# Output projection and gating dealt out among the attention units of the next token tile

## The chip, the cores and the metric

The kernel runs on one core of one Trainium2 chip. A core has TensorE (PE, with its weight loads shown apart as PEld), VectorE (DVE), ScalarE (ACT), GpSimd (POOL) and SyncE (SP), which here only issues transfers. Each engine works through its own instruction stream in order and waits on semaphores. The metric is the device time of one execution in microseconds, the median of several runs.

## The reference, cut to what matters

Two layers of a transformer-like block over 128 context tokens and 512 latent tokens, width 1024. In each layer:

```
mod = silu(cond) @ mod_w + mod_b                  # sh1, sc1, g1, sh2, sc2, g2
h = rms_norm(x, norm1_g) * (1 + sc1) + sh1
... = split_proj(h @ w_in)
o_a = recurrent scan;  o_g = global attention;  o_w = windowed attention with a sink
x = x + g1 * (concatenate([o_a, o_g, o_w]) @ w_out)     # what the change moves
h = rms_norm(x, norm2_g) * (1 + sc2) + sh2
x = x + g2 * moe(h)
```

The modulation rows differ between context (tile 0) and latent tokens (tiles 1 to 4). The context reads only itself; a latent tile's global attention reads five key tiles (four latent, one cached), its windowed attention three or four.

## The kernel before

Everything is float32. The 640 tokens are `NT` = 5 tiles of 128. A layer is one pass of a hardware loop and consists of blocks; all engines meet at a block's end. The block around the change is attention. Its work is 60 units, twelve for each token tile (2 kinds of attention x 2 key heads x 3 query heads), and `U` is 60. The order is written out by hand as steps 0 to 61, and all engines walk the same steps:

- PE (`score_pair`, L1012) on even steps makes the scores of units s and s+1; on each step it turns the probabilities of unit s-1 by transposes (`turn`, L1038) and multiplies those of unit s-2 by the values (`weigh`, L1051).
- DVE takes the row maximum of unit s (`maximum`, L1115 or L1119 with the mask), every four steps normalises a finished group of four units into `oall` (`outputs`, L1149 to L1151), and copies a part of the turned probabilities of unit s-1 out of PSUM (`copy_turned`, L1140). Four pieces of work on the scan's output (`scan_norm`) lie on steps 2, 4, 6 and 8.
- ACT makes the exponentials of unit s (L1081) and copies the other part (`copy_turned`, L1094).
- Before `weigh` begins a new group (steps 6, 10, 14, ..., that is 2 mod 4) PE waits until `outputs` has emptied the one PSUM bank that the groups share.

Eight more pieces of `silu(cond) @ mod_w` (numbers 4 to 11, `mod_rows`, L339, 64 matmuls each) are laid on steps 4, 10, 16, ..., 46 (`mod_at`), between `score_pair` and `turn`, in PSUM banks 6 and 7; DVE adds the bias (`mod_evac`, L1162). SP loads their 2 MB of weights in three buffers, the 4 MB of `w_out`, and at the end stores the finished rows to memory in two transfers, waits, and the block ends.

The next block is the projection. For each tile PE turns `oall` by eight transposes (L1225) into PSUM, ACT copies the 128x1024 result to `oT` (L1247), PE multiplies it by `w_out` in two halves of 512 columns, eight products each (L1237; each float32 product is recorded as two MATMULs, so 32 for a tile). DVE multiplies the 1024 columns with the gate rows `g1b` (L1258) and adds to `x` (L1262). Transposes of tile t+1 go ahead of the products of tile t; `oT`, `prod` and the PSUM banks are double. SP loads `g1b` at the block's start (L1209). The block after it begins with squares of `x` on ACT (L1340).

```
                    for step in range(U + 2):
                        if step < U and step % 2 == 0:
                            score_pair(step)
                        if step in mod_at:
                            ...
                        if 1 <= step <= U:
                            turn(step - 1)
                        if step >= 2:
                            weigh(step - 2)
```

Of the kernel before, what the change touches and what calls it, by code (L numbers as in the profile page):

```python
# [13 lines left out]
ALU = mybir.AluOpType  # L14
# [11 lines left out]
AH = 4  # L26
# [37 lines left out]
def program(nc, x_prompt, x_sample, cgk, cgv, cwk, cwv, state, c, c_ctx, mod_w, mod_b, norm1_g, norm2_g,  # L64
# [4 lines left out]
    with ctx:  # L69
# [89 lines left out]
        assert tt[0] <= scan0 + 6 * TOK  # L159
# [5 lines left out]
        oT = T[:, 0:2 * KC * P].rearrange("p (s k n) -> p s k n", s=2, k=KC)  # L165
        prod = T[:, 2048:2048 + 2 * D].rearrange("p (s n) -> p s n", s=2)
        g1b = T[:, scan0:scan0 + 2 * D].rearrange("p (s n) -> p s n", s=2)
# [120 lines left out]
        with nc.Fori(0, DEPTH) as layer:  # L288
# [29 lines left out]
            def by_group(a, cond):  # L318

                return a[cond:P:32]  # L320
# [98 lines left out]
            with nc.Block() as block:  # L419
# [504 lines left out]
            s_row2, s_mst, s_wo, s_hp, s_hq, s_hn, s_fill = (  # L924
                lsem(n) for n in ("mod_bias_load2", "mod_rows_stored", "wout_load", "scan_mean", "scan_rstd", "scan_norm",
# [39 lines left out]
            mod_at = {4 + 6 * i: MOD1 + i for i in range(NMOD - MOD1)}  # L965

            with nc.Block() as block:
                @block.sync
                def _(sp):
# [15 lines left out]
                    for cond in range(2):  # L985
                        sp.dma_start(mod_dram[cond, :].rearrange("(s g b) -> g s b", g=MODG, b=P),
                                     by_group(modrow2, cond)).then_inc(s_mst, 16)
                    sp.wait_ge(s_mst, 2 * 16)
# [10 lines left out]
                def _(pe):  # L999
# [56 lines left out]
                    for step in range(U + 2):  # L1056
                        if step < U and step % 2 == 0:
                            score_pair(step)
                        if step in mod_at:
                            n = mod_at[step]  # L1060
                            if n >= MOD1 + 2:
                                pe.wait_ge(s_mre, n - 1)
                            mod_rows(pe, n, 6 + n % 2).then_inc(s_mr, 1)
                        if 1 <= step <= U:
                            turn(step - 1)
                        if step >= 2:
                            weigh(step - 2)

                @block.scalar
                def _(act):  # L1070
# [25 lines left out]
                    for step in range(U + 2):  # L1096
                        if step < U:
                            exponential(step)
                        if 1 <= step <= U:
                            copy_turned(step - 1)  # L1100

                @block.vector
                def _(dve):
# [52 lines left out]
                    def mod_evac(n):  # L1156
# [5 lines left out]
                        ins = dve.tensor_tensor(r, PS[:, 6 + n % 2, 0:P], r, ALU.add)  # L1162
# [9 lines left out]
                    def scan_norm(part):  # L1172
# [6 lines left out]
                        elif part == 2:  # L1179
                            flow(dve.tensor_tensor(osum, osum, ga, ALU.mult))  # L1180
                        else:
                            dve.wait_ge(s_hq, 1)
                            flow(dve.tensor_tensor(oall[:, :, 0:AW].rearrange("p t (a d) -> p t a d", d=HD),
                                                   osum.rearrange("p t (a d) -> p t a d", d=HD),
                                                   hrs.unsqueeze(3).to_broadcast([P, NT, AH, HD]), ALU.mult))
# [3 lines left out]
                    for step in range(U + 3):  # L1189
                        if step < U:  # L1190
                            maximum(step)
                        if step >= 3 and (step - 3) % GU == GU - 1:
# [9 lines left out]
            s_gb, s_ot, s_ote, s_y, s_yp, s_yv = (  # L1202
                lsem(n) for n in ("gate_rows_load", "o_turned", "o_turned_evac", "y_done", "y_gated",
                                  "y_added"))

            def load_rows(sp, dst, at, s_sig):

                for cond in range(2):
                    sp.dma_start(dst[:, cond, :], mod_dram[cond, at * D:(at + 1) * D].partition_broadcast(P))\  # L1209
                      .then_inc(s_sig, 16)  # L1210

            with nc.Block() as block:
                @block.sync
                def _(sp):
                    load_rows(sp, g1b, 0, s_gb)

                @block.tensor
                def _(pe):
                    pe.wait_ge(s_wo, 16)

                    def turn(t):
                        if t >= 2:
                            pe.wait_ge(s_ote, t - 1)
                        for k in range(KC):
                            last = pe.transpose(PS[:, 2 * (t % 2) + k // 4, col(k % 4)], oall[:, t, col(k)], ident)  # L1225
                        last.then_inc(s_ot, 1)

                    turn(0)
                    for t in range(NT):
                        if t + 1 < NT:  # L1230
                            turn(t + 1)
                        pe.wait_ge(s_ote, t + 1)
                        if t >= 2:
                            pe.wait_ge(s_yp, t - 1)
                        for b in range(2):
                            for k in range(KC):
                                last = pe.matmul(PS[:, 4 + 2 * (t % 2) + b, :], oT[:, t % 2, k, :],  # L1237
                                                 wout[:, k, col(b, 512)], start=(k == 0), stop=(k == KC - 1))
                        last.then_inc(s_y, 1)

                @block.scalar
                def _(act):
                    for t in range(NT):
                        act.wait_ge(s_ot, t + 1)
                        if t >= 2:
                            act.wait_ge(s_y, t - 1)
                        act.activation(oT[:, t % 2, :, :].rearrange("p k n -> p (k n)"),  # L1247
                                       PS[:, 2 * (t % 2):2 * (t % 2) + 2, :].rearrange("p b n -> p (b n)"),
                                       ACT.Copy).then_inc(s_ote, 1)

                @block.vector
                def _(dve):
                    dve.wait_ge(s_gb, 2 * 16)
                    for t in range(NT):
                        dve.wait_ge(s_y, t + 1)
                        if t >= 2:
                            dve.wait_ge(s_yv, t - 1)
                        dve.tensor_tensor(prod[:, t % 2, :],  # L1258
                                          PS[:, 4 + 2 * (t % 2):6 + 2 * (t % 2), :].rearrange("p b n -> p (b n)"),
                                          g1b[:, 1 if t else 0, :], ALU.mult).then_inc(s_yp, 1)  # L1260
                        dve.wait_ge(s_yp, t + 1)
# [543 lines left out]
```

## Time and profile before

| | us |
|---|---|
| median of three runs (range) | 1830.77 (1828.58 to 1835.3) |
| the profiled execution | 1821.91 |
| span in the profile, first to last instruction | 1819.0 |
| end of the last `weigh` to the start of the next block, layer 1 / 2 | 78.87 / 78.88 |
| units of tile 2, layer 1 | 34.60 |
| units of tile 1, layer 1 | 45.00 |

A line of the timeline gives the start in us from the start of the span, the duration, engine, line, operation, output<-input, shape and count; in brackets stands the idle time of that engine just before, and what ended it. Neighbouring instructions of a kind are merged. The granted clock (PEclk) is the share of TensorE's full 2.4 GHz; it has two levels, 1.00 and 0.50 (1.2 GHz).

### The profile page before, as it was taken

To read this page: it belongs to the slowest core of one execution; us is meant where nothing else is said; L and a number is where in the kernel's file an instruction comes from. 1 tells how busy PE (TensorE), PEld (TensorE's weight loads), DVE (VectorE), ACT (ScalarE), POOL (GpSimd) and SP (SyncE) were. 2 spreads that over 40 slices of the span, in tenths; PEclk is the share of its full clock that TensorE was granted. 3 is DMA by queue.
4 is the path that set the end of the run, shared out by engine and by line. 5 is a ranking of instruction groups with operands and counts; after the bars stand their busy time and mean duration, and the time that the engine had idled before them with its cause. 6 is when DMAs were issued, how large, how long until landed. Compare 5 with 4: busy or idle time off the path is not lost. (4 is left out here: it accounts for less than half of the span.)

```text
span 1819.0 us, 22010 instructions
## 1 busy us (share of the span) xinstructions
PE 1469.5 (81%) x7971; PEld 929.6 (51%) x7972; DVE 625.1 (34%) x1352; ACT 359.4 (20%) x814; POOL 202.1 (11%) x151
## 2 busy tenths in 40 slices
PE   2799999698898559999039999987988964999940
PEld 2466556587753534444035755556877434444410
DVE  0236462545421421111411454635553134111123
ACT  2210012233311301111122000123332030111113
POOL 0114420100000010000210243110000000100010
PEclk9799999579899569999569999997896985999975
DMA  8211000825000369996380111027200034799833
GB/s 307 74 50 50 29 23 2 325 94 220 2 24 14 120 240 351 370 368 239 127 287 11 41 50 47 6 104 267 94 2 24 0 110 171 259 366 370 326 110 117
DMA packets 118648, 263.36 MB, mean 145 GB/s; under 512 B 10120, under 2 KB 27168, under 8 KB 118432
## 3 DMA queue, kind: packets, MB, share of 16 engines
q1 hardware_dynamic: 105600, 214.97, 33.3%
q0 software_dynamic: 8064, 29.36, 4.4%
q10 hardware_dynamic: 4896, 17.83, 2.4%
q8 instruction: 58, 0.95, 0.2%
q14 instruction: 30, 0.25, 0.0%
HBM read 230.88 MB, written 42.27 MB: 150 GB/s over the span
## 5 line engine op out<-in xcount | busy, mean ns | idle before, releaser
L638 PE MATMUL PS<-W,hT 128*128 128x512 f32 (+1 forms) x640 | 274.1, 555 | 0.0
L1587 PE MATMUL PS<-W,T 128*128 128x512 f32 x544 | 242.5, 599 | 4.5 <-ACT T L1629 4.5
L1587 PEld LDWEIGHTS PS<-W,T 128*128 128x128 f32 x544 | 104.3, 193 | 135.7 <-issue 130.0
L1051 PE MATMUL PS<-T 128*128 128x64 f32 x864 | 135.3, 308 | 27.4 <-DVE hT L1151 27.4
L1051 PEld LDWEIGHTS PS<-T 128*128 128x128 f32 x864 | 132.5, 232 | 32.0 <-issue 32.0
L638 PEld LDWEIGHTS PS<-W,hT 128*128 128x128 f32 x640 | 109.9, 189 | 74.5 <-issue 60.3
L1237 PE MATMUL PS<-W,T 128*128 128x512 f32 x320 | 139.7, 596 | 0.0
L1605 PE MATMUL PS<-W,T 128*128 128x512 f32 x272 | 126.0, 607 | 1.4 <-ACT T L1653 1.4
L810 DVE COPY_PREDICATED W<-levelmask,PS 128x512 f32<-128x512 uint8 (+2 forms) x96 | 77.6, 809 | 104.0 <-PE PS L579 103.8
L1012 PE MATMUL PS<-T 64*128 64x128 f32 (+3 forms) x480 | 90.7, 466 | 15.9 <-ACT T L1081 12.7
L542 PE MATMUL PS<-hT,W 128*128 128x512 f32 x192 | 100.3, 604 | 2.6 <-DVE hT L781 2.6
L1038 PE MATMUL PS<-cst,T 128*128 128x128 f32 x432 | 85.3, 324 | 16.3 <-ACT T L1081 8.2
L1237 PEld LDWEIGHTS PS<-W,T 128*128 128x128 f32 x320 | 60.9, 193 | 73.3 <-issue 73.3
L579 PEld LDWEIGHTS PS<-W 64*128 64x128 f32 x1120 | 69.0, 187 | 56.0 <-issue 38.9
L1675 DVE TENSOR_TENSOR T<-PS,T 128x256 f32<-128x256 f32 x34 | 14.5, 426 | 240.3 <-ACT T L1640 240.3
L508 PE MATMUL PS<-cst,T 128*128 128x128 f32 x80 | 19.1, 425 | 84.2 <-ACT T L663 84.2
L1081 ACT ACTIVATE T<-PS,small 128x640 f32<-128x640 f32 (+1 forms) x72 | 46.9, 651 | 194.2 <-DVE small L1126 158.9
L579 PE MATMUL PS<-W 64*128 64x128 f32 x1120 | 85.1, 287 | 0.0
L1115 DVE TENSOR_REDUCE small<-PS 128x1 f32<-128x640 f32 (+1 forms) x72 | 46.5, 646 | 105.5 <-PE PS L1012 105.3
L1671 DVE COPY T<-PS 128x1024 f32<-128x1024 f32 x34 | 41.7, 1226 | 119.4 <-PE PS L1605 119.4
L339 PE MATMUL PS<-W,condT 128*32 128x128 f32 x1536 | 63.0, 334 | 23.6 <-DMA W<-in_mod_w 18.8
L1545 POOL DMA_INDIRECT T<-h_rows,T x36 | 34.0, 944 | 427.7 <-PE PS L1577 323.9
(244 smaller groups left out, 1712.1 us busy)
## 6 DMA issues: line engine op xcount, KB each, us to landing
W<-in_w_gate_up SPq DMA_DIRECT2D x34, 2048.0 KB
W<-in_mod_w SPq DMA_DIRECT2D x24, 2048.0 KB, 12.2
W<-in_w_down SPq DMA_DIRECT2D x34, 1024.0 KB
y_rows<-T ACTq DMA_DIRECT2D x34, 512.0 KB, 9.2
y_rows<-cst SPq DMA_DIRECT2D x2, 7680.0 KB
W<-in_w_in SPq DMA_DIRECT2D x10, 1024.0 KB, 11.0
W<-in_w_in SPq DMA_DIRECT2D x4, 2048.0 KB, 7.9
W<-in_w_out SPq DMA_DIRECT2D x2, 4096.0 KB, 25.6
```

The source lines that it names most:

```text
L339: last = pe.matmul(PS[32 * g:32 * g + 32, bank, 0:P], condT[:, k, :], modw[:, n % 3, k, col(g)], start=(k == 0), stop=(k == KC - 1))
L542: pe.matmul(PS[:, bank, :], w, hT[:, k, 0:512], start=(k == 0), stop=(k == KC - 1))
L579: last = pe.matmul(PS[:, bank + r, col(2 * (tile - t) + f)], k_op[64 * r:64 * r + 64, d, f, col(tile)], rhs, start=True, stop=True)
L638: last = pe.matmul(PS[:, u % 4, 0:512 - at], hT[:, k, col(t)], ring[:, slot, k, at:512], start=(k == 0), stop=(k == KC - 1))
L810: dve.copy_predicated(query_side(Am[:, d, :, t:t + tiles, :, :].rearrange("p r t f n -> p r (t f n)"), lv, d), mask.to_broadcast([P, 4 * t ...
L1012: return pe.matmul(PS[:, score_bank(u) + n // 4, (n % 4) * P:(n % 4 + m) * P], qT[kv_rows, wnd, j, col(t)], kT[kv_rows, wnd, kt * P:(kt + ...
L1038: last = pe.transpose(PS[:, bank, col(at)], pr[units[u][1]][:, col(n)], ident)
L1051: last = pe.matmul(PS[:, 5, in_group(u) * HD:(in_group(u) + 1) * HD], prT[wnd][:, col(n)], v[:, kt, kv * HD:(kv + 1) * HD], start=(n == 0) ...
L1081: act.activation(pr[wnd][:, 0:n], src, ACT.Exp, bias=stat(nbias, u), scale=SCALE, accum_out=stat(rsum, u)).then_inc(s_ax, 1)
L1237: last = pe.matmul(PS[:, 4 + 2 * (t % 2) + b, :], oT[:, t % 2, k, :], wout[:, k, col(b, 512)], start=(k == 0), stop=(k == KC - 1))
L1587: last = pe.matmul(PS[:, 2 + par, :], hgT[:, par, k, :], w[:, k, :], start=(k == 0), stop=(k == KC - 1))
L1605: last = pe.matmul(PS[:, 6 + b, :], haT[:, par, col(f)], w[:, f, col(b, 512)], start=(f == 0), stop=(f == 1))
```

## The change

The projection block is gone. Its work for tile t is put into the steps of the next tile's units, starting at `window[t]` = 12 (t + 1) + 3, so at steps 15, 27, 39, 51 and, for the last tile, 63, after all units:

- `turn_out(t)` at step `window`: eight transposes into banks 6 and 7, and ACT's `copy_out` into the one `oT`, ahead of ACT's `copy_turned` of that step.
- `project(t, 0)` at `window` + 1 and `project(t, 1)` at `window` + 5: eight products each, into bank 6 and bank 7, between `score_pair` and `turn`. These are steps 16, 20; 28, 32; 40, 44; 52, 56; 64, 68.
- `gate_out(t, b)` on DVE at `window` + 5 and `window` + 9, after `maximum` and ahead of `copy_turned`: product and sum of 512 columns each. Steps 20, 24; 32, 36; 44, 48; 56, 60; 68, 72.
- The pieces of the modulation move from steps 4, 10, 16, 22, 28, 34, 40, 46 to 8, 13, 17, 22, 29, 34, 41, 46.
- SP loads `w_out` one place earlier, waits until pieces 4 and 5 are finished, stores those two, waits, loads `g1b`, and only then goes on with the weights of pieces 7 to 11; the other six rows are stored at the end.
- `oT`, `prod` and `g1b` get other places; `oT` and `prod` are single. A new semaphore `s_on` tells that the scan's part of `oall` is written.

```diff
-            mod_at = {4 + 6 * i: MOD1 + i for i in range(NMOD - MOD1)}
+            UT = U // NT
+            window = [UT * (t + 1) + 3 for t in range(NT)]
+            HALF = 4
+            LASTSTEP = window[-1] + 2 * HALF + 1
+            mod_at = {8: MOD1, 13: MOD1 + 1}
+            mod_bank = {MOD1: 6, MOD1 + 1: 7}
+            for i in range(3):
+                mod_at[window[i] + 2], mod_bank[MOD1 + 2 + 2 * i] = MOD1 + 2 + 2 * i, 7
+                mod_at[window[i] + 7], mod_bank[MOD1 + 3 + 2 * i] = MOD1 + 3 + 2 * i, 6
+            turn_at = {window[t]: t for t in range(NT)}
+            part_at = {window[t] + 1 + HALF * b: (t, b) for t in range(NT) for b in range(2)}
+            gated_at = {window[t] + HALF * (b + 1) + 1: (t, b) for t in range(NT) for b in range(2)}
...
                     load_mod(sp, MOD1 + 1)
+                    sp.dma_start(wout[:, :, :], w_out[layer].rearrange("(k p) n -> p k n", p=P)).then_inc(s_wo, 16)
                     load_mod(sp, MOD1 + 2)
-                    sp.dma_start(wout[:, :, :], w_out[layer].rearrange("(k p) n -> p k n", p=P)).then_inc(s_wo, 16)
+                    sp.wait_ge(s_mre, MOD1 + 2)
+                    store_mods(sp, MOD1, 2)
+                    sp.wait_ge(s_mst, 2 * 16)
+                    load_rows(sp, g1b, 0, s_gb)
                     for n in range(MOD1 + 3, NMOD):
                         load_mod(sp, n)
...
+                    def turn_out(t):
+                        pe.wait_ge(s_mre, mods_before(window[t]))
+                        pe.wait_ge(s_aev, G * (t + 1))
+                        if t == 0:
+                            pe.wait_ge(s_on, 1)
+                        else:
+                            pe.wait_ge(s_yp, 2 * t)
+                        for k in range(KC):
+                            last = pe.transpose(PS[:, 6 + k // 4, col(k % 4)], oall[:, t, col(k)], ident)
+                        last.then_inc(s_ot, 1)
+
+                    def project(t, b):
+                        if b == 0:
+                            pe.wait_ge(s_ote, t + 1)
+                            if t == 0:
+                                pe.wait_ge(s_wo, 16)
+                        else:
+                            pe.wait_ge(s_mre, mods_before(window[t] + 5))
+                        for k in range(KC):
+                            last = pe.matmul(PS[:, 6 + b, :], oT[:, k, :], wout[:, k, col(b, 512)],
+                                             start=(k == 0), stop=(k == KC - 1))
+                        last.then_inc(s_y, 1)
...
-                    for step in range(U + 2):
+                    for step in range(LASTSTEP):
                         if step < U and step % 2 == 0:
                             score_pair(step)
+                        if step in turn_at:
+                            turn_out(turn_at[step])
                         if step in mod_at:
-                            n = mod_at[step]
-                            if n >= MOD1 + 2:
-                                pe.wait_ge(s_mre, n - 1)
-                            mod_rows(pe, n, 6 + n % 2).then_inc(s_mr, 1)
+                            mod_side(step)
+                        if step in part_at:
+                            project(*part_at[step])
                         if 1 <= step <= U:
                             turn(step - 1)
...
+                    def gate_out(t, b):
+                        if (t, b) == (0, 0):
+                            dve.wait_ge(s_gb, 2 * 16)
+                        dve.wait_ge(s_y, 2 * t + b + 1)
+                        if t >= 1:
+                            dve.wait_ge(s_yv, 2 * (t - 1) + b + 1)
+                        dve.tensor_tensor(prod[:, b, :], PS[:, 6 + b, :], g1b[:, 1 if t else 0, col(b, 512)], ALU.mult)\
+                           .then_inc(s_yp, 1)
+                        dve.wait_ge(s_yp, 2 * t + b + 1)
+                        dve.tensor_tensor(x[:, t, col(b, 512)], x[:, t, col(b, 512)], prod[:, b, :], ALU.add).then_inc(s_yv, 1)
...
+                        if step in gated_at:
+                            gate_out(*gated_at[step])
                         if step in mod_at:
                             mod_evac(mod_at[step])
                         if 1 <= step <= U:
                             copy_turned(step - 1)
...
-            with nc.Block() as block:
-                @block.sync
-                def _(sp):
-                    load_rows(sp, g1b, 0, s_gb)
...
```

## Rows read from the trace of the kernel before

**Rows 1.** The page: span, and busy time, share and instructions of each engine.

```profile
span 1819.0 us, 22010 instructions
PE 1469.5 (81%) x7971; PEld 929.6 (51%) x7972; DVE 625.1 (34%) x1352; ACT 359.4 (20%) x814; POOL 202.1 (11%) x151
```

**Rows 2.** Windows: stretch, length, busy (x) per engine, granted clock, DMA.

```profile
core 0: us, PE busy (x) PEld busy (x) DVE busy (x) ACT busy (x) POOL busy (x), PEclk, DMA share, GB/s
351.10:396.10 45.00, 41.41 (x326) 35.81 (x327) 18.61 (x58) 12.98 (x39) 0.00 (x0) 0.66 0.40 141
396.10:430.70 34.60, 30.18 (x349) 27.67 (x349) 19.94 (x59) 14.07 (x40) 0.00 (x0) 1.00 0.70 265
...
508.65:587.52 78.87, 74.91 (x200) 35.89 (x200) 13.00 (x13) 5.12 (x5) 0.00 (x0) 0.98 0.04 14
...
1402.86:1481.74 78.88, 74.91 (x200) 35.90 (x200) 13.01 (x13) 5.12 (x5) 0.00 (x0) 0.98 0.04 14
```

**Rows 3.** Timeline of the projection block, layer 1: its start, second tile and end.

```profile
509.83 3.15 PE L1225 MATMUL PS<-cst,hT 128*128 128x128 f32 x16 [1.19 <-PEq L967]
511.31 1.02 ACT L1247 ACTIVATE T<-PS 128x1024 f32<-128x1024 f32 x1 [4.24 <-PE PS L1225]
...
512.78 14.40 PE L1237 MATMUL PS<-W,T 128*128 128x512 f32 x32
...
527.01 1.04 PE L1225 MATMUL PS<-cst,hT 128*128 128x128 f32 x8
...
527.89 13.90 PE L1237 MATMUL PS<-W,T 128*128 128x512 f32 x32
...
586.03 1.22 DVE L1262 TENSOR_TENSOR x<-x,T 128x1024 f32<-128x1024 f32 x1
...
587.56 1.06 ACT L1340 ACTIVATE T<-x 128x1024 f32<-128x1024 f32 x1 [29.23 <-PEq L1212]
```

**Rows 4.** Timeline of steps 24 to 26, layer 1, at full clock.

```profile
395.96 0.42 DVE L1140 COPY T<-PS 128x256 f32<-128x256 f32 x1
...
396.31 0.68 DVE L1119 CUSTOM_DVE_ANT_0 T<-PS,cst 128x512 f32<-128x512 f32 x1
...
397.27 0.74 PE L1038 MATMUL PS<-cst,T 128*128 128x128 f32 x5 [0.74 <-ACT T L1094]
...
397.90 0.19 ACT L1081 ACTIVATION_READ_ACCUMULATOR T<-T,small 128x1 f32 x1
...
398.55 1.34 PE L1012 MATMUL PS<-T 64*128 64x512 f32 x10
```

**Rows 5.** Waits in the units of tiles 1 to 4: total us, times, longest.

```profile
PE PS L1051 <- DVE hT L1151: 12.7, 9, 1.6
...
PE PS L1038 <- ACT T L1094: 3.9, 6, 0.7
...
PE PS L1038 <- ACT T L1094: 3.1, 5, 0.7
```

**Rows 6.** Windows at one granted clock, and sums of six at 0.50 per layer.

```profile
373.84:390.91 17.07, 17.07 (x127) 14.77 (x125) 5.32 (x17) 4.21 (x12) 0.00 (x0) 0.50 0.06 21
...
sum 58.03, PE 56.91 PEld 48.23 DVE 17.13 ACT 13.74 POOL 0.00; mean PE 9.48 PEld 8.04 DVE 2.85 ACT 2.29 POOL 0.00
...
sum 61.43, PE 60.30 PEld 52.75 DVE 18.93 ACT 14.93 POOL 0.00; mean PE 10.05 PEld 8.79 DVE 3.16 ACT 2.49 POOL 0.00
...
390.91:438.69 47.78, 41.26 (x444) 37.91 (x441) 27.76 (x83) 19.77 (x57) 0.00 (x0) 1.00 0.67 254
...
513.79:588.88 75.09, 70.95 (x184) 32.42 (x182) 12.24 (x10) 4.62 (x7) 0.00 (x0) 1.00 0.01 3
```

**Rows 7.** Timeline: the weighing that begins a group, step 18, layer 1.

```profile
373.33 1.91 PE L1051 MATMUL PS<-T 128*128 128x64 f32 x10 [1.48 <-DVE hT L1151]
```

**Rows 8.** Groups by line and form: a DVE product out of PSUM.

```profile
L1675 DVE TENSOR_TENSOR T<-PS,T 128x256 f32<-128x256 f32 x34 | 14.5, 426 | 240.3 <-ACT T L1640 240.3
```

**Rows 9.** The page's DMA issues: KB each, median us to landing.

```profile
W<-in_w_out SPq DMA_DIRECT2D x2, 4096.0 KB, 25.6
```

**Rows 10.** Timeline: the first piece of the modulation in attention, layer 1.

```profile
327.50 3.64 PE L339 MATMUL PS<-W,condT 128*32 128x128 f32 x64 [1.02 <-DMA W<-in_mod_w]
```

More of the change, by code:

```diff
@@ L158, in program @@
         sm = carve1(WK)
-        assert tt[0] <= scan0 + 6 * TOK
+        assert tt[0] <= scan0 + 6 * TOK - D
         tt[0] = tail
@@ L963, in stat, with mods_before, load_rows, store_mods @@
                 return a[:, n:n + 1]
-            mod_at = {4 + 6 * i: MOD1 + i for i in range(NMOD - MOD1)}
+            s_gb, s_ot, s_ote, s_y, s_yp, s_yv = (
+                lsem(n) for n in ("gate_rows_load", "o_turned", "o_turned_evac", "y_done", "y_gated", "y_added"))
+            UT = U // NT
[7 more added lines that the diff above has]
+                mod_at[window[i] + 7], mod_bank[MOD1 + 3 + 2 * i] = MOD1 + 3 + 2 * i, 6
+            assert sorted(mod_at.values()) == list(range(MOD1, NMOD))
+            turn_at = {window[t]: t for t in range(NT)}
+            part_at = {window[t] + 1 + HALF * b: (t, b) for t in range(NT) for b in range(2)}
+            gated_at = {window[t] + HALF * (b + 1) + 1: (t, b) for t in range(NT) for b in range(2)}
+            def mods_before(step):
+                return max([MOD1] + [n + 1 for s, n in mod_at.items() if s < step])
+            def load_rows(sp, dst, at, s_sig):
+                for cond in range(2):
+                    sp.dma_start(dst[:, cond, :], mod_dram[cond, at * D:(at + 1) * D].partition_broadcast(P))\
+                      .then_inc(s_sig, 16)
+            def store_mods(sp, first, n):
+                for cond in range(2):
+                    sp.dma_start(mod_dram[cond, (first - MOD1) * MODW:(first - MOD1 + n) * MODW]
+                                 .rearrange("(s g b) -> g s b", g=MODG, b=P),
+                                 by_group(modrow2[:, first - MOD1:first - MOD1 + n, :], cond)).then_inc(s_mst, 16)
             with nc.Block() as block:
@@ L984, in _ @@
                     sp.wait_ge(s_mre, NMOD)
[L985 to L988, printed above, removed]
+                    store_mods(sp, MOD1 + 2, NMOD - MOD1 - 2)
+                    sp.wait_ge(s_mst, 4 * 16)
                     sp.wait_ge(s_fill, 16)
@@ L1057, in _, with mod_side @@
+                    def mod_side(step):
+                        n = mod_at[step]
+                        if n == MOD1 + 3 or n == MOD1 + 5 or n == MOD1 + 7:
+                            pe.wait_ge(s_yp, n - MOD1 - 2)
+                        mod_rows(pe, n, mod_bank[n]).then_inc(s_mr, 1)
+                    for step in range(LASTSTEP):
                         if step < U and step % 2 == 0:
                             score_pair(step)
+                        if step in turn_at:
+                            turn_out(turn_at[step])
@@ L1094, in copy_turned, with copy_out @@
                             act.activation(prT[units[u][1]][:, m:n], PS[:, 4, 0:n - m], ACT.Copy).then_inc(s_aca, 1)
-                    for step in range(U + 2):
+                    def copy_out(t):
+                        act.wait_ge(s_ot, t + 1)
+                        if t >= 1:
+                            act.wait_ge(s_y, 2 * t)
+                        act.activation(oT.rearrange("p k n -> p (k n)"), PS[:, 6:8, :].rearrange("p b n -> p (b n)"),
+                                       ACT.Copy).then_inc(s_ote, 1)
+                    for step in range(window[-1] + 1):
                         if step < U:
                             exponential(step)
+                        if step in turn_at:
+                            copy_out(turn_at[step])
                         if 1 <= step <= U:
@@ L1199, in _ @@
                             scan_norm(norm_at[step])
[L1202 to L1210, printed above, removed]
-            with nc.Block() as block:
-                @block.sync
-                def _(sp):
-                    load_rows(sp, g1b, 0, s_gb)
[L1217 to L1261, printed above, removed]
-                        dve.tensor_tensor(x[:, t, :], x[:, t, :], prod[:, t % 2, :], ALU.add).then_inc(s_yv, 1)
```

26 lines of the change are left out of this document (14 added, 12 removed).

## The prediction

> **What bounds the kernel now.** I first read the page's busy times: PE is busy for 81% of the span, the others for a third or less [rows 1]. Then I cut each layer into its stages by windows. The projection block is 78.9 us in either layer, PE busy for 74.9 us of it at a granted clock of 0.98 [rows 2]: a solid run of products that nothing holds up. The units before it are PE-bound too, though less plainly. With the clock at 1.00 the twelve units of tile 2 take 34.60 us, PE busy for 30.18; with the clock at 0.66 those of tile 1 take 45.00, PE busy for 41.41 [rows 2]. So PE carries both stages, and moving work from one to the other gains nothing by itself. A gain can come from three places only: idle time of PE among the units, the ends of the block, and the clock.
>
> The waits among the units say where PE idles. Per layer nine waits of up to 1.6 us for the group's output (12.7 us), six of about 0.7 us for ACT's copy in layer 1 and five in layer 2 [rows 5]. Last I read the granted clock as the stretches in which it stays at one level. Among the units of tiles 1 to 4 there are six at 0.50 (1.2 GHz) in each layer, 58.0 and 61.4 us together, with PE busy nearly all through; in a long one at 1.00, PE is busy for 41.26 of 47.78 us [rows 6]. They begin shortly after a wait for a group's output: one such wait ends at 373.33 [rows 7], the clock is at 0.50 from 373.84 [rows 6].
>
> **The change part by part**, both layers counted.
>
> The end of the block. Before, a layer's stage runs 78.87 us from the last weighing [rows 2]. After, only tile 4 is left. Its first product can start where the first product starts now, 512.78: transposes and ACT's copy stand before it in the same way, and I count nothing for the barrier of 1.19 us that goes, since the wait for the last group's output, now hidden in part behind it, takes its place [rows 3]. The products last 14.40 us, to 527.2 [rows 3]. DVE's first half is hidden behind the second eight products. A half of 512 columns costs 0.69 us on DVE, interpolated between 426 ns for 256 columns [rows 8] and 1.22 us for 1024 [rows 3]; so product and sum of the second half end 1.5 us later, at 528.7. The next block begins 0.3 us after (586.03 + 1.22 to 587.56 [rows 3]): 529.0 instead of 587.5. That takes out 58.5 us a layer, 117.0 us in all; bounds 115 and 120, by the barrier.
>
> The four other tiles among the units. One tile's eight transposes and 32 MATMULs take 0.88 + 13.90 = 14.8 us, or 15.1 us by the starts of two neighbouring blocks of products (512.78 to 527.89) [rows 3]. I take 14.8, since weight loads can run ahead when the neighbour is another matmul; 4 x 2 x 14.8 = +118.4 us at full clock, 121 at the upper end. ACT's copy of 1.02 us lies on an odd step, ahead of one further score pair, and the products come on the next step, so PE doesn't wait for it; without that cover it would be 1.3 us a tile, 10 us.
>
> Idle time filled. The products stand on steps that are 0 mod 4, ahead of the 0.7 us wait for ACT's copy, and cover it on steps 20, 32, 44, 52 and 56, some of which were free before: I take five of the eleven waits at their mean of 0.64 us [rows 5], -3.2 us (bounds 0 and -7). The longer waits for a group's output are on steps that are 2 mod 4; there the three modulation pieces on steps 22, 34 and 46 stay as they were, and nothing new is put.
>
> The gating on DVE. The first half runs on steps 20, 32, 44, 56, while PE is at the second eight products: free. The second runs on steps 24, 36 and 48 with no products on PE. In step 24 it stands ahead of the copy at 395.96 and of the next maximum at 396.31 [rows 4], and its two instructions with a wait between them take 1.4 us. The copy would end at 397.8, so PE's turning, at 397.27 now, starts 0.5 us later; the exponentials of unit 25 would end 1.4 us later than 398.09, so the scores that start at 398.55 wait until 399.5 [rows 4]. That is 1.0 us each, 6 x 1.0 = +6.0 us (0 where the clock is low and PE late anyway, 1.4 each at most: 8.4). On step 60 it hides behind the last weighings.
>
> The modulation pieces. Moving the first from step 4 to 8 takes out a wait of 1.02 us for its weights in layer 1 [rows 10]; moving the second from step 10, where PE waits for other engines, to step 13, where it is the bound, puts up to 3.64 us [rows 10] on the path less what it hides. I take 0 for both together, between -2 and +4.
>
> Transfers. SP now waits for pieces 4 and 5 (step 13), stores them, waits, and loads the gate rows ahead of the weights of pieces 7 to 11. The first of these is used on step 22, a projected half and some 25 us of units later. `w_out` takes 25.6 us to land [rows 9] and is used from step 16, some 45 us after its issue. Both are covered; the price if not is in the rivals. The new waits on PE (output of the group, rows of the modulation, the last gating) stand behind work that is done two or more steps earlier by this order.
>
> Sum without the clock: -117.0 + 118.4 - 3.2 + 6.0 + 0 = +4.2 us.
>
> The clock. One us at 0.50 costs between 0.34 us (tile 1 against tile 2: 10.4 us for the (1 - 0.66) / 0.5 x 45.0 = 30.6 us at half clock, though tile 1 has somewhat less work [rows 2]) and 0.5 us; I take 0.4. Nine waits a layer go with six falls; nine stay, so I keep six. Before, a stretch at half clock lasts 119.5 / 12 = 10.0 us on average, up to 17 in the rows shown [rows 6]. After, products follow two steps behind eight of the nine waits. From the fall to the first product I estimate 3.5 us of work at full clock (a score pair at 1.34 us, a turning at 0.74 [rows 4], the rest of two weighings), 7 us at half; and when products began at half clock in the projection block, the clock was back at 1.00 1.0 us later (512.78 [rows 3] to 513.79 [rows 6]). So 8 us a stretch: 12 x 8 = 96 us, 23.5 less, x 0.4 = -9.4 us.
>
> Forecast: +4.2 - 9.4 = -5.2 us. The profiled execution took 1821.91 us, its span and 2.9 around it; the median of the three is 8.9 above. I put the difference on the median: 1830.8 - 5.2 = 1826 us (1817 for an execution like the profiled one).
>
> **The rivals.**
>
> The clock comes back sooner. If the transposes on the step before already raise it, or if fewer waits lead to a fall, stretches of 4 us would remain: 48 us instead of 119.5, 71.5 x 0.4 = -28.6; with +4.2, -24 us, 1806. For it: the clock rose 1.0 us after the first products. Against it: the waits that go with the falls all stay.
>
> The clock gains nothing: 1830.8 + 4.2 = 1835. For it: falls depend on where a wait lies, and pieces of the modulation on steps 16, 28 and 40 ended some of the stretches already.
>
> The second half of the gating makes the clock fall (the slower side). On steps 24, 36, 48 PE's idle time grows from 0.74 to 1.3 us and gets another 0.5 to 1 us before the next scores, as much as the waits of up to 1.6 us after which the clock falls now. If it always falls there, a pair of units more runs at half clock until step 28, 40 or 52: some 5 us of work, 10 instead of 5, six times 5 = 30 us on top. 1835 + 30 - 9 for the stretches that still shorten = 1856. It decides from the point at which more than two of the six fall, and where the clock was low anyway it does nothing.
>
> Products at half clock. In the block the clock stands at 1.00 for 75.09 us [rows 6]; in pieces of 7 us each could start at 1.2 GHz and keep it. If each of the sixteen halves ran half its products so, 16 x 3.5 = 56 us: 1835 + 56 = 1891. The row on the rise within 1.0 us speaks against it. The Trainium skill (TensorE: Matmul & The Clock Gate, "Loop structure matters more than you think") asks for the opposite of this change: products kept back to back, with the next iteration's following at once. By that rule the result would be this one; the rows of before don't settle it, since no product there lies among units.
>
> The change doesn't do what it says: a transfer (`w_out`, the gate rows, a modulation weight) ends last on steps 16 to 22, and PE stands for 10 us or more in each layer: 1826 + 20 = 1846.
>
> **How the numbers follow.** What can be told from no change is about 0.5%, 9.2 us: faster below 1821.6, slower above 1839.9. Chances: forecast 0.48 (its own range 1815 to 1837 by the bounds of the terms; a fifth of it below 1821.6), clock sooner 0.22, no clock gain 0.12, gating 0.11, products at half clock 0.03, transfers 0.04. Faster: 0.22 + 0.10 = 0.32; slower: 0.11 + 0.03 + 0.04 = 0.18; the rest, 0.50, is neither. The range for 8 in 10 takes in most of the first rival and of the slower ones near by: 1804 to 1849.
>
> **What would show it.** Right: from the last weighing to the next block 20 to 21 us; stretches at half clock of some 8 us that end with the first products of a half; DVE's second half ahead of a PE wait of about 1.3 us on steps 24, 36, 48; a half in 6.9 us. Wrong: half-clock time among the units above 120 or below 60 us in all; PE waiting for a DMA at a product; halves that take 10 us or more.

## The result and the profile after

The changed kernel took 1800.2 us (median of five, 1795.0 to 1808.0) against 1830.8 before: ratio 0.984, 95% interval [0.981, 0.988]. In a second series, on another occasion, it was 1802.2 us, ratio 0.987 [0.982, 0.991]. It is faster by 1.3 to 1.6%, about five times the forecast 5 us, and below the stated range.

The two profiled executions stand closer together, 1819.0 and 1805.9 us of span (the changed one is the slowest of its five). The stage from the first exponential of attention to the block behind the projection is 22 us shorter for both layers (266.9 + 266.6 us before, 257.2 + 254.2 after), and 31.5 us in the mean of two profiles of each kernel (533.5 and 545.8 before, 511.4 and 504.8 after). Outside it the changed kernel's are longer by some 9 us, behind the second layer's projection (337.3 and 337.8 us before, 346.0 and 346.0 after). This goes with the clock: there the changed kernel has 148 us at half clock in both profiles, the kernel before 128. `mods_moved` below, the kernel before with one line changed, has 346.1 there too, with 151 us at half clock, so I can't put this down to the change, and what moves it was not followed. In the second pair of profiles another 8.5 us lie between the two layers' stages (621.4 us before, 629.9 after), again with more half-clock time (143 and 164 us); the first pair has 2 us there.

Windows of the changed kernel, layer 1: tile 2's units with tile 1's projection among them, then from the last weighing to the next block; the last row is that end in layer 2. Columns as in [rows 2].

```profile
400.50:451.40 50.90, 46.58 (x390) 36.29 (x389) 22.71 (x64) 15.24 (x40) 0.00 (x0) 0.97 0.56 214
...
554.46:576.07 21.61, 17.81 (x40) 8.24 (x40) 3.53 (x7) 1.02 (x1) 0.00 (x0) 0.84 0.00 0
...
1437.79:1459.90 22.11, 18.23 (x40) 8.46 (x40) 3.53 (x7) 1.08 (x2) 0.00 (x0) 0.80 0.00 1
```

The stage behind the units fell from 78.9 us [rows 2] to 21.6 and 22.1. Tile 2 went from 34.60 us [rows 2] to 50.90.

PE's waits among the units of tiles 1 to 4 in layer 1 (total us, times, longest), to set beside [rows 5]:

```profile
PE PS L1087 <- DVE hT L1227: 12.9, 9, 1.5
PE PS L1074 <- DVE T L1216: 3.6, 3, 1.3
PE PS L1048 <- ACT T L1148: 0.3, 1, 0.3
```

The nine waits for a group's output are all still there. The waits for ACT's copy are gone; three longer ones for DVE's copy have come, at the second gatings.

The granted clock: the six stretches at half clock in layer 1 and their sum, and the sum of the six in layer 2, up to the last weighing, to set beside [rows 6].

```profile
354.17:357.59 3.42, 3.42 (x20) 3.42 (x17) 0.56 (x1) 1.85 (x5) 0.00 (x0) 0.50 0.99 276
374.65:384.89 10.24, 10.24 (x33) 6.80 (x33) 3.25 (x9) 2.07 (x6) 0.00 (x0) 0.50 0.22 81
408.79:412.20 3.41, 3.41 (x19) 3.41 (x17) 0.56 (x1) 1.83 (x5) 0.00 (x0) 0.50 0.00 0
459.99:466.81 6.82, 6.82 (x28) 5.70 (x27) 1.54 (x3) 1.70 (x5) 0.00 (x0) 0.50 0.00 0
511.19:514.60 3.41, 3.41 (x18) 3.41 (x18) 0.30 (x2) 1.58 (x4) 0.00 (x0) 0.50 0.00 0
531.67:538.49 6.82, 6.82 (x14) 3.35 (x14) 2.60 (x5) 1.02 (x3) 0.00 (x0) 0.50 0.00 0
sum 34.12, PE 34.12 PEld 26.09 DVE 8.80 ACT 10.05 POOL 0.00; mean PE 5.69 PEld 4.35 DVE 1.47 ACT 1.68 POOL 0.00
...
sum 28.89, PE 28.81 PEld 25.65 DVE 8.11 ACT 8.80 POOL 0.00; mean PE 4.80 PEld 4.27 DVE 1.35 ACT 1.47 POOL 0.00
```

As many stretches as before, twelve, but 63 us instead of 119.5. The first, third and fifth, behind steps 14, 26 and 50, last 3.4 us, and the first is over at 357.59, while the first product begins at 359.07:

```profile
352.87 1.30 PE L1087 MATMUL PS<-T 128*128 128x64 f32 x10 [1.48 <-DVE hT L1227]
354.01 1.76 PE L1101 MATMUL PS<-cst,hT 128*128 128x128 f32 x8
355.56 1.27 PE L1074 MATMUL PS<-cst,T 128*128 128x128 f32 x5
356.63 1.24 PE L1087 MATMUL PS<-T 128*128 128x64 f32 x6
357.80 1.34 PE L1048 MATMUL PS<-T 64*128 64x512 f32 x10
359.07 3.27 PE L1112 MATMUL PS<-W,T 128*128 128x512 f32 x7
```

That is the timeline of PE on steps 14 to 16 (the view ends within the last line; the whole half takes 7.13 us). Only the eight transposes (L1101) and the units' own work lie between the wait and the rise of the clock. So the products can't have ended this stretch. The experiments follow this up.

### The profile page after: what moved, and what is told of

Its sections match the earlier page's. It is cut to its first block and busy times, and to the rows that moved or that the text cites. A ratio compares the mean times of both kernels' runs of the same rounds, so it can differ in the third digit from the quotient of the medians.

```text
span 1805.9 us, 22024 instructions
## 1 busy us (share of the span) xinstructions
PE 1456.1 (81%) x7971; PEld 914.6 (51%) x7972; DVE 627.8 (35%) x1372; ACT 359.9 (20%) x814; POOL 203.0 (11%) x151
## 5 line engine op out<-in xcount | busy, mean ns | idle before, releaser
L1613 PE MATMUL PS<-W,T 128*128 128x512 f32 x544 | 244.8, 604 | 4.5 <-ACT T L1655 4.5
L1112 PE MATMUL PS<-W,T 128*128 128x512 f32 x320 | 152.1, 632 | 2.2 <-ACT T L1167 2.2
L1087 PE MATMUL PS<-T 128*128 128x64 f32 x864 | 124.1, 289 | 29.9 <-DVE hT L1227 29.8
L1087 PEld LDWEIGHTS PS<-T 128*128 128x128 f32 x864 | 120.2, 213 | 34.9 <-issue 34.7
L1631 PE MATMUL PS<-W,T 128*128 128x512 f32 x272 | 126.9, 611 | 1.5 <-ACT T L1679 1.5
L1216 DVE COPY T<-PS 128x384 f32<-128x384 f32 (+1 forms) x120 | 53.8, 448 | 139.1 <-PE PS L1074 138.3
L1048 PE MATMUL PS<-T 64*128 64x128 f32 (+3 forms) x480 | 80.7, 425 | 16.1 <-ACT T L1148 12.6
L1074 PE MATMUL PS<-cst,T 128*128 128x128 f32 x432 | 79.2, 306 | 12.9 <-DVE T L1216 7.7
L509 PE MATMUL PS<-cst,T 128*128 128x128 f32 x80 | 18.5, 415 | 85.1 <-ACT T L664 85.1
```

The source lines that it names most:

```text
L1048: return pe.matmul(PS[:, score_bank(u) + n // 4, (n % 4) * P:(n % 4 + m) * P], qT[kv_rows, wnd, j, col(t)], kT[kv_rows, wnd, kt * P:(kt + ...
L1074: last = pe.transpose(PS[:, bank, col(at)], pr[units[u][1]][:, col(n)], ident)
L1087: last = pe.matmul(PS[:, 5, in_group(u) * HD:(in_group(u) + 1) * HD], prT[wnd][:, col(n)], v[:, kt, kv * HD:(kv + 1) * HD], start=(n == 0) ...
L1112: last = pe.matmul(PS[:, 6 + b, :], oT[:, k, :], wout[:, k, col(b, 512)], start=(k == 0), stop=(k == KC - 1))
L1216: dve.tensor_copy(prT[units[u][1]][:, 0:m], PS[:, 3, 0:m]).then_inc(s_acv, 1)
L1613: last = pe.matmul(PS[:, 2 + par, :], hgT[:, par, k, :], w[:, k, :], start=(k == 0), stop=(k == KC - 1))
```

## The experiments

Two numbers are used for each kernel beside the median. Half-clock time among the units (from the first exponential of tile 1 to the end of the last weighing, both layers, in its one profile), and half-clock time of a whole run, 2 x (1 - mean granted clock) x span, as a mean over the kernel's runs, since one profile is one draw. The runs of before in the other two series have 493 (23) and 489 (17).

| kernel | median us | ratio to before [95%] | among units, one profile | whole run, mean (runs) |
|---|---|---|---|---|
| before | 1826.4 | | 119 and 151 | 492 (13) |
| changed | 1800.2 | 0.984 [0.981, 0.988] | 65 and 52 | 444 (5), 450 (6) |
| mods_moved | 1830.2 | 1.003 [1.000, 1.007] | 80 | 512 (10) |
| one_product_each | 1718.2 | 0.942 [0.935, 0.949] | 65 | 472 (4) |
| one_turn_each | 1817.8 | 0.996 [0.993, 0.999] | 99 | 492 (10) |
| turns_only | 1816.9 | 0.994 [0.992, 0.997] | 64 | 452 (10) |
| two_group_banks | 1774.9 | 0.971 [0.964, 0.978] | 27 | 392 (4) |
| products_on_the_waits | 1754.8 | 0.961 [0.954, 0.968] | 0 | 396 (4) |
| second_gate_moved | 1787.0 | 0.978 [0.975, 0.982] | 43 | 416 (6) |
| quarters | 1726.0 | 0.946 [0.942, 0.950] | 0 | 360 (4) |

Over three series of 13, 23 and 17 runs of the kernel before, a run was slower by 0.33, 0.30 and 0.33 us for each us more of half-clock time.

**The kernels once more.** `before_again` is the kernel before, `after_again` the changed one.

> The kernel before once more, for the spread of its half-clock time: 1826 us by the runs so far, half-clock time among the units of tiles 1 to 4 between 90 and 150 us in this profile, and about 0.35 us of time for each us of half-clock time from run to run.

> The changed kernel once more, beside the kernel before on the same chip: 1800 us, ratio 0.984, half-clock time among the units of tiles 1 to 4 between 50 and 75 us in this profile (62 in the first), with the stretches behind steps 14, 26, 38 and 50 ending by step 15, 27, 39, 51.

Measured: 1829.0 us and 1802.2 us. The second profile of before has 151 us at half clock among the units, and one of its stretches is much longer than any in the first profile. Its second and its fourth stretch in layer 1:

```profile
371.80:388.90 17.10, 17.10 (x127) 14.79 (x127) 5.34 (x17) 4.21 (x12) 0.00 (x0) 0.50 0.06 21
474.20:518.60 44.40, 40.96 (x165) 33.53 (x164) 13.69 (x41) 11.46 (x30) 0.00 (x0) 0.50 0.07 25
```

The fourth runs from step 51 through tile 4, which has no modulation piece, into the projection block; layer 2 has another of 44.4 us at the same place. Eight stretches make up these 151 us, where the first profile has twelve and 119.5, though over the whole run the two agree (496 and 493 us). So the prediction's "10.0 us on average" is one draw of a length that varies from run to run.

**The modulation pieces alone** (`mods_moved`).

```diff
-            mod_at = {4 + 6 * i: MOD1 + i for i in range(NMOD - MOD1)}
+            mod_at = {s: MOD1 + i for i, s in enumerate((8, 13, 17, 22, 29, 34, 41, 46))}
```

> The kernel before with the eight modulation pieces on the new steps (8, 13, 17, 22, 29, 34, 41, 46) and nothing else of the change. Theory (the gain is the clock's: products two steps behind the waits for a group's output end the half-clock stretches early): no products move here, so 1831 us as before, between 1827 and 1835, half-clock time among the units of tiles 1 to 4 about 120 us as in the profile of before. Rival (the new places of the modulation pieces shorten those stretches): 1800 to 1815 us, half-clock time 60 to 80 us.

Measured: 1830.2 us. Their places explain nothing of the gain. The 80 us of its profile alone, from the fastest of its ten runs, would have misled; the mean of ten runs has 20 us more half-clock time than before, not less.

**What starts the stretches** (`two_group_banks`). The kernel before, but PE no longer waits for the output of the group just finished:

```diff
-                        if u % GU == 0 and g >= 1:
-                            pe.wait_ge(s_aev, g)
+                        if u % GU == 0 and g >= 2:
+                            pe.wait_ge(s_aev, g - 1)
...
-                            last = pe.matmul(PS[:, 5, in_group(u) * HD:(in_group(u) + 1) * HD],
+                            last = pe.matmul(PS[:, 5 + g % 2, in_group(u) * HD:(in_group(u) + 1) * HD],
...
-                            mod_rows(pe, n, 6 + n % 2).then_inc(s_mr, 1)
+                            mod_rows(pe, n, 7).then_inc(s_mr, 1)
```

> The kernel before with two PSUM banks in turn for the groups' outputs (bank 6 beside 5; the modulation pieces all in bank 7), so that PE no longer waits for the output of the group before. Theory (this wait starts the half-clock stretches): nine waits of 1.4 us per layer go, about half of each coming back as the 0.7 us wait for ACT's copy: -12 us; half-clock time among the units falls from 120 to below 50 us: -28 us; together 1790 us, between 1775 and 1800. Rival (the units' own light load lets the clock fall, the wait only happens to stand there): -12 us, 1819 us, half-clock time 100 us or more.

Measured: 1774.9 us. Its waits of PE in the units of tiles 1 to 4, layer 1, and a window of the same units:

```profile
PE PS L1038 <- ACT T L1094: 8.6, 12, 0.7
PE PS L1038 <- DVE T L1140: 4.1, 6, 0.8
...
PE PS L1038 <- ACT T L1081: 1.6, 1, 1.6
...
364.70:482.20 117.50, 105.00 (x1088) 93.63 (x1086) 69.05 (x204) 49.02 (x142) 0.00 (x0) 1.00 0.33 122
```

The nine waits of 1.4 us and the six of 0.7 [rows 5], 16.6 us, have turned into 18 waits of 0.7 us, 12.7 us in all, and now the clock stays at 1.00 for 117.5 us without a break. What remains at half clock is one stretch at the start of tile 1 in each layer. In layer 1 it begins, as in the kernel before, behind a wait of 1.6 us for ACT's exponentials (the third line); in layer 2 it comes over from tile 0. Idle time in pieces of 0.7 us doesn't bring the clock down here; pieces of 1.4 us do, though not each time. With some 4 us of idle time less in layer 1, most of the gain of 52 us came from the clock.

**Products left out** (`one_product_each`).

```diff
-                        for k in range(KC):
+                        kept = KC if t == NT - 1 else 1
+                        for k in range(kept):
```

> The changed kernel, but each half of tiles 0 to 3 makes only the first of its eight products (the output is left incomplete); tile 4 is whole. 16 halves of 7.13 us lose seven eighths: 99.8 us at full clock. Rival (a half costs what it lasts, the clock does its own thing): 1800 - 100 = 1700 us, half-clock time among the units 62 us as in the changed kernel. Theory (the products shorten the half-clock stretches): these go back to 120 us or more, about 58 us more at 0.4 us each = +23, so 1723 us, between 1715 and 1732.

Measured: 1718.2 us, 82 us less, nearer to the theory's 1723. But the half-clock time speaks against it: 65 us among the units in this profile, as in the changed kernel; and over whole runs 472 us, about half-way between the changed kernel's 447 and 492 before. With seven of eight products gone, a good part of the shortening is still there. The theory's time fits, but its mechanism doesn't carry it: at 0.33 us each, 25 us more at half clock make 8 of the 18 us that are missing from the 100, and the rest was not followed. That led to the next two.

**The transposes alone** (`turns_only`). The kernel before with eight idle transposes on steps 15, 27, 39, 51:

```diff
+                        if step in (15, 27, 39, 51):
+                            pe.wait_ge(s_mre, max(n + 1 for s, n in mod_at.items() if s < step))
+                            for k in range(KC):
+                                pe.transpose(PS[:, 6 + k // 4, col(k % 4)], cst[:, 128:256], ident)
```

> The kernel before with eight transposes of a constant tile more on steps 15, 27, 39 and 51, into banks 6 and 7, where the changed kernel has those of the output projection; their result is not used. In the trace of the changed kernel the half-clock stretches behind steps 14, 26, 38 and 50 end before the first product begins. Theory A (the transposes on the next step end them): the stretches behind these four steps, 65 us of the 119 in the profile of before, shrink to 3.4 us each, about 44 us less at 0.36 us, -16 us, against +8.4 us for 8 x 1.05 us of transposes: 1818 us; half-clock time among the units 70 to 85 us. Theory B (only products end them): +8.4 us, 1835 us, half-clock time as before.

Measured: 1816.9 us; with 8 us of work added, it is faster than before by 0.6%. Its half-clock stretches behind steps 14, 18, 38 and 50 in layer 1:

```profile
358.33:361.75 3.42, 3.42 (x19) 3.42 (x17) 0.56 (x1) 0.89 (x4) 0.00 (x0) 0.50 0.32 117
371.99:389.05 17.06, 17.06 (x127) 14.74 (x127) 5.35 (x16) 4.21 (x12) 0.00 (x0) 0.50 0.04 14
436.84:440.25 3.41, 3.41 (x19) 3.41 (x18) 0.56 (x1) 1.00 (x4) 0.00 (x0) 0.50 0.02 5
474.39:477.80 3.41, 3.41 (x18) 3.29 (x18) 0.56 (x1) 0.46 (x2) 0.00 (x0) 0.50 0.00 0
```

Where transposes follow on the next step, 3.4 us; where none do (the second), 17.1, as before. The stretches at these steps in layer 2 are less clean (10.2 us, begun ahead of step 14, and 6.8 twice), but the sum went from 119 and 151 to 64, and over whole runs from 492 to 452 us, nearly as far as in the changed kernel.

**The transposes left out** (`one_turn_each`).

```diff
-                        for k in range(KC):
+                        for k in range(KC if t == NT - 1 else 1):
                             last = pe.transpose(PS[:, 6 + k // 4, col(k % 4)], oall[:, t, col(k)], ident)
```

> The changed kernel with only the first of the eight transposes of tiles 0 to 3 on steps 15, 27, 39 and 51 (the output is left incomplete); the products stay. Removed work: 8 x 0.9 us = -7 us. Theory A (these transposes end the stretches behind steps 14, 26, 38 and 50): the stretches last on to the first products, 7 to 8 us instead of 3.4 to 6.8 (mean 4.3), half-clock time among the units up by 20 to 30 us, +9 us: 1802 us. Theory B (the products alone end them): half-clock time as in the changed kernel, 1793 us.

Measured: 1817.8 us. With 7 us of work less it is 16 to 18 us slower than the changed kernel. PE on steps 14 to 16, and the window of the stretch:

```profile
353.37 1.30 PE L1087 MATMUL PS<-T 128*128 128x64 f32 x10 [1.48 <-DVE hT L1227]
354.50 0.28 PE L1101 MATMUL PS<-cst,hT 128*128 128x128 f32 x1
354.62 0.97 PE L1074 MATMUL PS<-cst,T 128*128 128x128 f32 x5
355.38 1.38 PE L1087 MATMUL PS<-T 128*128 128x64 f32 x6
356.70 2.50 PE L1048 MATMUL PS<-T 64*128 64x512 f32 x10
359.13 8.42 PE L1112 MATMUL PS<-W,T 128*128 128x512 f32 x16
...
354.90:361.70 6.80, 6.80 (x23) 4.54 (x22) 1.54 (x3) 2.28 (x7) 0.00 (x0) 0.50 1.02 348
```

Now the scores take 2.50 us and the half 8.42 instead of 7.1, as it starts at half clock. Over whole runs the half-clock time is back at 492 us, the figure of before. Among the units of its one profile it is 99 us, between the changed kernel's 65 and 52 and the 119 and 151 of before. So without the transposes the products, on the same steps, shorten a part of the stretches at most; the transposes gave about half of the whole-run shortening with one product in each half (`one_product_each`) and nearly all of it beside the old projection block (`turns_only`).

**Dense work on the waits** (`products_on_the_waits`). Halves and modulation pieces on the steps on which PE waits:

```diff
-            mod_at = {8: MOD1, 13: MOD1 + 1}
+            mod_at = {10: MOD1, 14: MOD1 + 1}
...
-                mod_at[window[i] + 2], mod_bank[MOD1 + 2 + 2 * i] = MOD1 + 2 + 2 * i, 7
-                mod_at[window[i] + 7], mod_bank[MOD1 + 3 + 2 * i] = MOD1 + 3 + 2 * i, 6
+                mod_at[window[i] + 5], mod_bank[MOD1 + 2 + 2 * i] = MOD1 + 2 + 2 * i, 7
+                mod_at[window[i] + 11], mod_bank[MOD1 + 3 + 2 * i] = MOD1 + 3 + 2 * i, 6
...
-            part_at = {window[t] + 1 + HALF * b: (t, b) for t in range(NT) for b in range(2)}
+            part_at = {window[t] + 3 + HALF * b: (t, b) for t in range(NT) for b in range(2)}
...
-            gated_at = {window[t] + HALF * (b + 1) + 1: (t, b) for t in range(NT) for b in range(2)}
+            gated_at = {window[t] + 4 + HALF * b: (t, b) for t in range(NT) for b in range(2)}
```

> The changed kernel with everything dense put on the steps on which PE waits for a group's output (2 mod 4), between the scores and the turning: halves on steps 18, 22, 30, 34, ... instead of 16, 20, 28, 32, ..., modulation pieces on steps 10, 14, 20, 26, 32, 38, 44, 50, gating behind DVE's copy on the odd steps 19, 23, .... Theory (these waits start the half-clock stretches): of the nine that lay open per layer none is left: 18 x 1.4 = 25 us of idle time go, of which the 0.7 us waits on the steps 0 mod 4 come back (ten or so, 7 us), the six late gatings give 6 us, and half-clock time among the units falls from 62 to below 20 us, 17 us: 1800 - 41 = 1759, between 1750 and 1775. Rival (falls come from the light load of the units between the dense pieces, wherever these stand): idle time goes, half-clock time stays near 60 us: 1776 us or more.

Measured: 1754.8 us. PE's waits in the units of layer 1, and the window of those units:

```profile
PE PS L1074 <- ACT T L1161: 6.1, 9, 0.7
PE PS L1074 <- ACT T L1148: 1.6, 1, 1.6
...
347.00:526.90 179.90, 172.39 (x1428) 129.86 (x1428) 87.13 (x242) 58.80 (x160) 0.00 (x0) 1.00 0.31 112
```

The waits for a group's output are hidden, and the units of four tiles run at 1.00 throughout. The mechanism and the sum both held. The second gating was moved as well, behind DVE's copy; the next run shows what that alone is worth.

**The second gating moved** (`second_gate_moved`): behind DVE's copy on step 21, 33, 45 (`late_at = {window[t] + 6: (t, 1)}`) instead of ahead of it on 24, 36, 48.

> The changed kernel with DVE's gating of each second half on step 21, 33, 45 behind its copy instead of 24, 36, 48 ahead of it. Theory (there it holds up the copy and the next maximum by 1.4 us, and PE by 1 us): six times 1.0 to 1.3 us, 1793 us, and PE's wait of 1.2 us for DVE's copy on steps 25, 37, 49 back at 0.7. Rival (PE's wait only moves to the next group's output): 1800 us.

Measured: 1787.0 us; PE's waits on those steps are back at 0.7. That is twice the expected gain; the half-clock time of a run fell by some 30 us as well. In its profile there is no stretch left at the end of tile 4, where the changed kernel has 17.1 us in layer 2, and the end of the block runs at the full clock:

```profile
547.28:566.18 18.90, 15.06 (x40) 6.86 (x40) 3.53 (x7) 1.02 (x2) 0.00 (x0) 1.00 0.00 1
```

**Cut finer** (`quarters`): `products_on_the_waits` with four products on each of steps 18, 20, 22, 24 and so on; modulation pieces and gatings move with them.

```diff
+            part_at = {window[t] + 3 + HALF * b + 2 * q: (t, b, q) for t in range(NT) for b in range(2) for q in range(2)}
...
+                        for k in range(4 * q, 4 * q + 4):
```

> The kernel with everything dense on the waits, but the halves cut in two again: four products on each of steps 18, 20, 22, 24 (and so on by twelves), modulation pieces on 10, 14, 16, 26, 28, 38, 40, 50, so that nearly each even step has something dense between the scores and the turning. Theory (the 0.7 us waits for ACT's copy, nine in each layer, are left open on the steps 0 mod 4 that have nothing dense): all but one or two per layer go, 15 x 0.74 = 11 us: 1744 us, half-clock time among the units below 5 us. Rival (each cut costs as much as it fills, the pipeline of TensorE starting anew 16 times): 1755 us or more.

Measured: 1726.0 us, ratio 0.946, the fastest kernel that does the whole work. PE's waits in the units of layer 1 and a window of them:

```profile
PE PS L1074 <- ACT T L1153: 1.6, 1, 1.6
PE PS L1074 <- ACT T L1166: 0.7, 1, 0.7
...
344.50:518.50 174.00, 171.29 (x1428) 128.75 (x1428) 86.95 (x241) 59.23 (x162) 0.00 (x0) 1.00 0.32 121
```

One wait of 0.7 us is left of nine. Up to the last weighing the units of tiles 1 to 4 take 6.5 us less than in `products_on_the_waits` in each layer (172.9 and 179.4 us), where the filled waits would give 5 to 6. The end of the block runs at the full clock, 18.9 us instead of 21.6, which gives 5 us more in two layers. The other 10 of the 29 us, in other stages with 25 us less half-clock time in the profile, were not followed.

## Why the prediction was wrong

- The end of the block: 58.5 us a layer expected, 57.3 and 56.8 measured (78.9 less 21.6 and 22.1). That it came so near is partly luck: at the full clock this end takes 18.9 us (`second_gate_moved`), so 60.0 us would have gone, and 2.7 to 3.2 us came back as the transposes and first products ran at half clock.
- Projection among the units: 14.8 us a tile with 1 us for the gating. Tile 2 rose by 16.3 us, with one 3.4 us stretch at half clock in it. Right.
- Idle time: all eleven waits for ACT's copy are gone, 7.0 us, where I took five, 3.2 us. Three in each layer have become waits for DVE's copy, which are told next.
- The second gating: PE's wait of 0.74 us on step 25 [rows 4] became 1.27, and the next scores wait 0.30 more:

```profile
400.42 0.68 DVE L1269 TENSOR_TENSOR T<-PS,T 128x512 f32<-128x512 f32 x1
...
401.14 0.69 DVE L1272 TENSOR_TENSOR x<-x,T 128x512 f32<-128x512 f32 x1
...
401.75 0.42 DVE L1216 COPY T<-PS 128x256 f32<-128x256 f32 x1
...
402.27 0.74 PE L1074 MATMUL PS<-cst,T 128*128 128x128 f32 x5 [1.27 <-DVE T L1216]
...
403.93 1.34 PE L1048 MATMUL PS<-T 64*128 64x512 f32 x10 [0.30 <-ACT T L1148]
```

  0.83 us instead of 1.0: right as a direct cost. With the eleven waits it makes 7.8 us in two layers, where the prediction comes to 9.8. That it also makes the clock fall, which I had as the slower rival, is partly so: in the two profiles of the changed kernel three stretches begin behind such a wait (one wait ends at 1287.65, the clock falls at 1289.43), but each lasts 3.4 us; and with this gating moved a run has some 30 us less at half clock (`second_gate_moved`), which is 10 us of time at 0.33 us each, not 30.
- Modulation pieces: 0 expected. `mods_moved` gave 1.003 [1.000, 1.007], some 4 us, within the bounds.
- Transfers: no wait of PE for one at a product.
- **The clock: this step failed.** That the waits for a group's output start most of the stretches held, though not all: the first in layer 1 of before, at 353.36, stands behind PE's wait for ACT's exponentials, `352.08 0.76 PE L1038 MATMUL PS<-cst,T 128*128 128x128 f32 x5 [1.59 <-ACT T L1081]`. That twelve start after as before held too, against the first profile of before. The price of 0.4 us was near enough: 0.30 to 0.33 from run to run, 0.4 behind the second layer's projection (8.5 us for 20). The failing term is the length of a stretch, 8 us, and under it the sentence that the products end them. I let the stretch run on until the products two steps behind, and passed over the eight transposes on the step between as mere cost of 1 us. They end it, in 3.4 us mostly: of the 14 stretches that begin behind the waits of steps 14, 26, 38 and 50 in the changed kernel's two profiles, 13 last 3.4 us and one 6.8. Behind the waits of steps 18 and 54, where products alone follow two steps later, five stretches last 6.8 us in the mean, near my 8. Over all twelve the mean is five us instead of eight (63 us). And before was counted from one profile, 119.5 us, where the second has 151. So 135 us became 58 in the mean of two profiles each: 77 us of half-clock time went instead of 23.5. At the price of 0.4 us that is -31 instead of -9.4, and with +4.2 it is -27; the stage fell by 31.5, the medians of runs by 24 and 31. Over whole runs the half-clock time fell by 45 us only, since outside the stage the profiles of the changed kernel have more of it (325 and 329 us, against 317 and 288), with the 9 us told of above and 8.5 more in the second pair; that part stays open.
- The rivals: the first named the transposes ("if the transposes on the step before already raise it") and gave 1806. It had a chance of 0.22 for want of a row in which transposes stand alone behind such a wait; there was one: in the projection block the clock rose at 513.79, after sixteen transposes and two products, and I gave that to the products.
- The Trainium skill (TensorE: Matmul & The Clock Gate, "Loop structure matters more than you think") shows products kept back to back, and I read it as speaking against this change. No run here bears that reading out: cut into sixteen quarters among the units they ran at 1.00, and the cut version is the fastest. The bad case of that section, a long wait for a transfer before each matmul, doesn't occur here. The same page ("Part 4: PE-mode transpose") says that the full clock doesn't engage for TensorE's transpose mode. `turns_only` and `one_turn_each` show that eight float32 transposes in a row, made as `pe.transpose` and recorded as MATMULs, shortened the stretches; whether they run in that mode the records don't tell.

## What to carry to other kernels

Where the granted clock drops among PE-bound work, look for the wait just ahead of each drop, and put independent dense work on that step, ahead of the waiting instruction: it hides the wait and the clock never falls (half-clock time among the units 65 to 0 us, 1800 to 1755 us; the second gating moved with it, which by itself gave 13 us), whereas dense work a step or two later only shortens what has begun. Count every dense piece that a change brings, transposes too, at the place where it stands. And take the half-clock time of before from several runs, as one profile of the same kernel gave 119 and another 151 us.

## What the runs showed that was not expected

Eighteen waits of 0.7 us, 12.7 us in layer 1, left the clock at full speed for 117.5 us, while nine of 1.4 us, the same 12.7 us beside six short ones, went with six drops. One longer wait alone need not do it: in `products_on_the_waits` PE waits 1.6 us for ACT's exponentials at the start of tile 1, and the clock stays at 1.00. One us of half-clock time was worth 0.30 to 0.33 us over 53 runs of one kernel, less than the half that the clock ratio suggests.
